# Two edits to a one-core fp32 transformer kernel: the first mixer's convolution and steps dealt anew, and the RWKV projection's third weight unit held apart

## What is computed

```python
proj = h @ w_in[l] + b_in[l]
q, k, v, gb, gc, xs = jnp.split(proj, ...)       # 512, 128, 128, 512, 512, 512 columns
q, k = rope(q), rope(k)
y_attn = sliding_window_attention(q, k, v, attn_sinks[l])   # blocks of 128, window 128, 8 heads on 2
y_conv = gc * causal_dwconv3(gb * xs, conv_w[l])            # three taps over time
y = jnp.concatenate([rms_norm(y_attn, ...), rms_norm(y_conv, ...)], axis=-1)
x = x + g1 * (y @ w_o[l])
```

## Time and profile before

| | us |
|---|---|
| median of 3 runs | 2073.39 |
| lowest, highest | 2070.76, 2075.92 |
| the profiled execution, its own time | 2070.89 |
| its span, first to last instruction | 2069.2 |
| TensorE busy in the span | 1973.0 (95%) |
| VectorE, ScalarE, GpSimd busy | 1064.3, 777.8, 252.5 |
| mean granted TensorE clock | 0.968 of full |

### The profile page before, as it was taken

The page is one execution under the profiler, slowest core; times in us unless marked ns, Lnnn a source line. Parts: engine busy times, 40 slices in busy tenths (PEclk is TensorE's granted clock), DMA queues, the critical chain, the costliest instruction groups (busy, mean ns, idle before and its releaser), DMA issues.

```text
span 2069.2 us, 35297 instructions
## 1 busy us (share of the span) xinstructions
PE 1973.0 (95%) x14503; PEld 1577.7 (76%) x14503; DVE 1064.3 (51%) x1567; ACT 777.8 (38%) x1242; POOL 252.5 (12%) x282
## 2 busy tenths in 40 slices
PE   6999899999999999799999999999989999999997
PEld 5767678888886677677777788888867878888886
DVE  6776775455324645687753744442255564444223
ACT  4333433333222335576643423222245443232221
POOL 1100000000014000322311211111100021111110
PEclk8998999999999999899999999999999999999998
DMA  8544323333332132000003133333222223333321
GB/s 309 164 132 122 92 72 93 100 92 112 101 92 73 52 92 85 6 10 7 7 27 102 44 102 98 96 113 97 81 64 79 82 72 102 92 100 100 111 84 41
DMA packets 311057, 181.09 MB, mean 88 GB/s; under 512 B 16381, under 2 KB 303763, under 8 KB 310932
## 3 DMA queue, kind: packets, MB, share of 16 engines
q1 hardware_dynamic: 305506, 162.29, 26.3%
q0 software_dynamic: 4608, 16.78, 2.6%
q10 hardware_dynamic: 818, 0.21, 0.0%
HBM read 177.16 MB, written 2.10 MB: 87 GB/s over the span
## 4 chain that ended last, share of the span: by engine, by line
PE 85%; DVE 8%; ACT 3%; issue 3%; ACTq 1%; POOL 0%; DVEq 0%; POOLq 0%
PE bank L258 22%; PE bank L260 22%; PE bank L259 22%; PE bank L2221 4%; DVE x L1399 1%; PE bank L2734 1%; ACT whi L236 1%; PE bank L1256 1%; PE bank L2728 1%; PE bank L1258 1%; PE bank L1257 1%; PE bank L562 1%; PE bank L2835 1%; DVE wlo L243 1%; PE bank L2006 1%
## 5 line engine op out<-in xcount | busy, mean ns | idle before, releaser
L243 DVE TENSOR_TENSOR wlo<-raw,whi 128x1024 fp32r<-128x1024 f32 (+1 forms) x254 | 331.1, 1304 | 665.3 <-ACT whi L236 665.1
L236 ACT ACTIVATE whi<-raw 128x1024 fp32r<-128x1024 f32 (+1 forms) x254 | 284.1, 1119 | 664.2 <-PE bank L260 657.9
L258 PE MATMUL bank<-fh_hi,whi 128*128 128x512 f32 x991 | 387.7, 391 | 0.9 <-DVE fh_lo L483 0.5
L259 PE MATMUL bank<-fh_lo,whi 128*128 128x512 f32 x991 | 386.3, 390 | 0.0
L260 PE MATMUL bank<-fh_hi,wlo 128*128 128x512 f32 x991 | 386.2, 390 | 0.0
L258 PEld LDWEIGHTS bank<-fh_hi,whi 128*128 128x128 f32 x991 | 186.4, 188 | 42.2 <-DVE fh_lo L483 1.8
L259 PEld LDWEIGHTS bank<-fh_lo,whi 128*128 128x128 f32 x991 | 186.5, 188 | 39.0 <-issue 0.5
L260 PEld LDWEIGHTS bank<-fh_hi,wlo 128*128 128x128 f32 x991 | 186.4, 188 | 38.9
L258 PE MATMUL bank<-f_hi,whi 128*128 128x512 f32 x528 | 205.7, 390 | 0.0
L260 PE MATMUL bank<-f_hi,wlo 128*128 128x512 f32 x528 | 205.4, 389 | 0.0
L259 PE MATMUL bank<-f_lo,whi 128*128 128x512 f32 x528 | 205.4, 389 | 0.0
(11 more groups left out here) (478 smaller groups left out, 3223.8 us busy)
## 6 DMA issues: line engine op xcount, KB each, us to landing
raw<-in_w_up_dram SPq DMA_DIRECT2D x44, 512.0 KB, 3.7
raw<-in_ffn_w_gate_dram SPq DMA_DIRECT2D x44, 512.0 KB, 3.7
raw<-in_ffn_w_up_dram SPq DMA_DIRECT2D x44, 512.0 KB, 3.7
raw<-in_ffn_w_down_dram SPq DMA_DIRECT2D x32, 704.0 KB, 4.2
late<-in_ada_w_dram POOLq DMA_DIRECT2D x32, 512.0 KB, 4.1
raw<-in_rwkv_w_rkv_dram SPq DMA_DIRECT2D x24, 512.0 KB, 3.4
raw<-in_w_down_dram SPq DMA_DIRECT2D x16, 704.0 KB, 4.2
early<-in_ada_w_dram SPq DMA_DIRECT2D x16, 512.0 KB, 14.2
```

What stands on the lines that cost most here:

```text
L236: act.activation(halves_of(at)[0][:, 0:kts * P], raw_unit(at, kts), ACT.Copy).then_inc(hi_ready, 1)
L243: dve.tensor_tensor(lo[:, 0:kts * P], raw_unit(at, kts), hi[:, 0:kts * P].bitcast(F32), ALU.subtract)\
L258: pe.matmul(dst, hi, rhs_hi(k), start=first and k == 0, stop=False)
L259: pe.matmul(dst, hi, rhs_lo(k), start=False, stop=False)
```

## The change

**First mixer.** (1) TensorE runs the first four tiles of unit 6 (`AHEAD`) before it transposes v and before the first scores; the wait of a group's first unit for its bank is loosened to match (`N_PRE - 1 + part`). (2) The other 92 tiles are dealt over the 16 steps by `step_start`: 5 or 6 to a step, and the third units now end 3, 2, 1 and 0 tiles before the end of steps 3, 7, 11 and 15. (3) VectorE's convolution is cut in product, taps and gate, and dealt around the next softmax: product ahead of the split; taps 0 and 1 between the softmax's first and second half; tap 2 and gate behind the second half. (4) Where a unit ends less than two tiles before its step's end (`ends_late`: steps 0, 4, 11), the low split goes behind the first half of the softmax.

**RWKV projection.** Unit 2 gets a place of its own (`w_third`, in the first half of what `y_all` kept). ScalarE splits it in the last round, behind the split of the seventh output tile; VectorE behind the last state. In `Project` the splits move up by one: at o = 0 that of unit 3 (free once unit 1 is done), at o = 1 that of unit 4 (free once unit 0 is done), none at o = 2, and the rest as before.

```diff
             elif part < 2:
-                pe.wait_ge(prj_ready, N_PRE)
+                pe.wait_ge(prj_ready, N_PRE - 1 + part)
...
     def dve_in(dve, u):
         split_lo(dve, first[u + 2])
-        at = at_in[u]
-        if u >= N_PRE and (u - N_PRE) % 3 == 2:
...
+    def conv_product(dve, j):
+        dve.wait_ge(unit_done, at_in[N_PRE + 3 * j + 2].count)
+        dve.wait_ge(gb_ready, j + 1)
+        wait(dve, conv_done, j - 1)
+        if j == 0:
+            dve.wait_ge(rope_done, 5)
+        dve.scalar_tensor_tensor(cbuf[:, j % 2, 2:T + 2], bank[MIX[2]][:, :], v("b_in", 10 + j), gb_sb[:, j % 2, :],
+                                 ALU.add, ALU.mult).then_inc(conv_p, 1)
+    def conv_tap(dve, j, w):
+        c, acc = cbuf[:, j % 2, :], cacc[:, j % 2, :]
+        if w == 0:
             dve.wait_ge(conv_p, j + 1)
+            dve.tensor_scalar(acc, c[:, 0:T], v("conv_w", j), None, ALU.mult).then_inc(conv_t, 1)
+        else:
+            dve.wait_ge(conv_t, 3 * j + w)
+            dve.scalar_tensor_tensor(acc, c[:, w:T + w], v("conv_w", 4 * w + j), acc, ALU.mult, ALU.add)\
+               .then_inc(conv_t, 1)
+    def conv_gate(dve, j):
+        dve.wait_ge(conv_t, 3 * j + 3)
+        dve.scalar_tensor_tensor(y_cv[:, j, :], bank[MIX[1]][:, :], v("b_in", 6 + j), cacc[:, j % 2, :],
+                                 ALU.add, ALU.mult).then_inc(conv_done, 1)
...
-    KS = (N_IN - N_PRE) * KD // len(STEPS)
+    AHEAD = 4
+    def step_start(i):
+        return AHEAD + ((N_IN - N_PRE) * KD - AHEAD) * i // len(STEPS)
...
-        tiles = [divmod(s, KD) for s in range(i * KS, (i + 1) * KS)]
+        tiles = [divmod(s, KD) for s in range(step_start(i), step_start(i + 1))]
...
+    def ends_late(i, u):
+        return step_start(i + 1) - (u + 1 - N_PRE) * KD < 2
...
+        pe_in(pe, N_PRE, range(AHEAD))
         pe_rotate(pe, N_PRE - 1)
         pe_scores(pe, 0)
...
         for i in range(len(STEPS)):
+            j, softmax = conv_of(i), i + 1 < len(STEPS)
+            if j is not None:
+                conv_product(dve, j)
             for u in ended(i):
-                dve_in(dve, u)
-            if i + 1 < len(STEPS):
+                if not (softmax and ends_late(i, u)):
+                    dve_in(dve, u)
+            if softmax:
                 dve_softmax_a(dve, i + 1)
+            for u in ended(i):
+                if softmax and ends_late(i, u):
+                    dve_in(dve, u)
+            if j is not None:
+                conv_tap(dve, j, 0)
+                conv_tap(dve, j, 1)
+            if softmax:
                 dve_softmax_b(dve, i + 1)
+            if j is not None:
+                conv_tap(dve, j, 2)
+                conv_gate(dve, j)
             ada_accumulate(dve, LATE_STEP[i])
...
-        sbs(part, "y_all", [P, KD, T])
+        w_third = sbs(part, "w_third", [P, 2, KD * P], F32R)
+        sbs(part, "y_late", [P, KD // 2, T])
...
                 if j:
                     act_split_y(act, j - 1)
+                if j == KD - 1:
+                    act.wait_ge(ys_ready, KD // 2)
+                    split_hi(act, out_tm.units[2], free=out_tm.at0.plus(-1))
...
                 dve_state(dve, j, 7)
+                if j == KD - 1:
+                    split_lo(dve, out_tm.units[2])
...
+        def splits_at(self, o):
+            if self.early and o < 2:
+                return self.units[o + 3], self.units[1 - o]
+            if self.early and o == 2 or o >= KD - 2:
+                return None
+            return self.units[o + 2], self.units[o]
...
             for o in range(KD):
-                at = self.at0.plus(o)
-                if o < KD - 2:
-                    split_hi(act, at.plus(2))
-                else:
+                at = self.units[o]
+                if self.splits_at(o):
+                    nxt, free = self.splits_at(o)
+                    split_hi(act, nxt, free=free)
+                if o >= KD - 2:
                     for nxt in self.after[o - KD + 2]:
                         split_hi(act, nxt, free=self.at0)
                 if o == KD - 2:
                     root_table(act)
                 act.wait_ge(unit_done, at.count)
                 if o < KD - 1:
                     act.activation(self.o[:, o, :], bank[o % 2][:, :], ACT.Copy).then_inc(o_ready.sem, 1)
```

More of the change, by code:

```diff
@@ L1030, in dve_in @@
         split_lo(dve, first[u + 2])
-        at = at_in[u]
-        if u >= N_PRE and (u - N_PRE) % 3 == 2:
[L1033 to L1041, removed]
-            dve.wait_ge(conv_p, j + 1)
-            conv_taps(dve, acc, c, lambda w: v("conv_w", 4 * w + j), conv_t, 3 * j)
-            dve.scalar_tensor_tensor(y_cv[:, j, :], bank[MIX[1]][:, :], v("b_in", 6 + j), acc,
-                                     ALU.add, ALU.mult).then_inc(conv_done, 1)
@@ L1047, in build @@
[L1047 to L1056, removed]
+    conv_t = sem("conv_t")
@@ L1198, in ended, with conv_of @@
         return [u for u, ks in pieces(i) if ks[-1] == KD - 1]
+    def ends_late(i, u):
+        return step_start(i + 1) - (u + 1 - N_PRE) * KD < 2
+    def conv_of(i):
+        return next(((u - N_PRE) // 3 for u in ended(i) if (u - N_PRE) % 3 == 2), None)
     def pe_mixer1(pe):
@@ L3103, in __init__ @@
             self.end = at0.plus(KD)
+            self.units = [at0.plus(o) for o in range(KD)]
+            if early:
+                self.units[2].held = w_third[:, 0, :], w_third[:, 1, :]
             self.o = mem
@@ L3142, in dve @@
             for o in range(KD - 2):
-                split_lo(dve, self.at0.plus(o + 2))
+                if self.splits_at(o):
+                    split_lo(dve, self.splits_at(o)[0])
             for units in self.after:
@@ L3160, in pe @@
                 if o < KD - 1:
-                    unit_products(pe, self.at0.plus(o), KD, bank[o % 2][:, :], hi, lo, True, True)
+                    unit_products(pe, self.units[o], KD, bank[o % 2][:, :], hi, lo, True, True)
             for ks in (range(KD - 1), range(KD - 1, KD)):
```

## The result

| | kernel before | changed kernel |
|---|---|---|
| median of the runs, us | 2072.06 (13 runs, 2066.73 to 2078.83) | **2054.48** (13 runs, 2049.84 to 2070.27) |
| profiled execution: its time, its span, us | 2070.89, 2069.2 | 2062.55, 2060.8 |
| ratio of the times | | **0.9923**, 95% interval 0.9908 to 0.9938 |

The change takes 17.6 us off, 0.77%. The 95% interval of the ratio stands for a gain of 12.8 to 19.1 us. The forecast was 2055.3, and its cases reached from 2050 to 2062. The profiled execution is one of the long ones of its own kernel, 8 us above its median, so its span can't be set against the other's as a whole. What can be compared is the stretch that was changed. I measure it from the first product of the last rotation to the output projection's first product: 214.90 - 84.61 = 130.29 us before, 199.02 - 88.14 = 110.88 after. **The mixer is 19.4 us shorter.**

A forecast was written before the change was run, and what follows sets the result against it. TensorE's idle and low-clock time bounds the kernel, with VectorE limiting the gain: 17.9 us in the mixer plus 0.2 in the RWKV projection, 18.1, from the median 2073.39 to 2055.3. Range 2050 to about 2058, to 2062 with half of rival 2.

The forecast's parts named there:

- The bound: First mixer: TensorE's idle and low-clock time can give back 19.9 us; VectorE, running continuously, limits the gain to 17.9.
- Four tiles ahead: First stretch, before step 0: twelve products fill 2.7 of 2.95 us idle, the clock stays high, 5.2 us gained.
- The price of 5.23 us: First stretch: twelve products at the low clock take 5.23 us and vanish; if the clock falls, only some 2.7 gained.
- VectorE's sum: First mixer: VectorE's instructions added up from softmax 2 at 100.9, less 4.7 hidden, end at 196.1; gain 17.9.
- The 2.09 from the last accumulation to the projection: Mixer's end: the output projection's first product comes 2.09 us behind the gate, as before, now at 197.0.
- Short waits of TensorE: First mixer: 2.0 us reappears as waits for probabilities and transposed copy, after steps 4, 5, 12 and 13.
- Rival 2: First mixer: the clock eats part; first stretch and short waits lose some 7 us, time 2062; chance 0.20.
- Rivals 3 and 4: Mixer: 3, probabilities stay late, no change within 0.3% (0.03); 4, waits in most steps, low clock, 2092 (0.02).
- the working on the queues: First mixer's queues: later weight loads are covered by four buffers; DMA engines busy 0.23 to 0.28 of the stalled stretches.
- Part three: RWKV projection's third unit: gain 0.2 us in place of 1.95, since unit 2 waits for bank 0's copy on ScalarE.
- The total: Whole kernel: 17.9 for the mixer plus 0.2 for the RWKV projection, 18.1 us, forecast 2055.3.

## Why the prediction was right, point by point

**The bound** was read rightly: TensorE's idle and slow time was what could be won, and VectorE's chain was what limited it. Of 4.4 us of added instructions 4.2 came through.

**Four tiles ahead.** The step "TensorE is then idle for only about 0.5 us before the scores" held: 0.40. The clock stayed at 1.00, and the slow products vanished. The stretch is as long as before (4.62 us), so all that the twelve products took later is gained. The price of 5.23 us holds only where the clock falls as it did in the first profile; without the tiles the loss was 5.3 in one place and 1.6 in a second, and in another execution of the kernel before nine products were slow and not twelve. A term of this kind has a range that one profile doesn't show.

**VectorE's sum.** From the first scores to the start of the last accumulation I had 194.9 - 89.23 = 105.7; measured, 196.94 - 92.76 = 104.2. The sum was 1.5 too long, and the gain from that profile 19.4 instead of 17.9. The mis-sized terms are these. The convolution's product is followed by an instruction that doesn't need it after 0.66 us, four times (116.03 to 116.69), where I had 0.78 from a place where the tap waits for it. Splits take 1.14 (109.59 to 110.73), not 1.18, eleven times. Together that is 0.9. What is hidden behind the exponentials is 5.2 in place of 4.7: 1.3 for the first convolution, 1.27 (not 1.0) for the second, 1.47 (not 1.25) in step 11, 1.13 for the split of step 4. Softmax 2 starts 0.16 earlier after the first scores than I had it. Against this stands 0.18 of a wait for the scores of softmax 10. That leaves 0.1. The 2.09 from the last accumulation to the projection was exact (2.08).

**Short waits of TensorE**, "a few tenths to 1.3 us each, after steps 4, 5, 12 and 13": their kind was right, and so was their sum (2.0 for p_t), but not their places. There are three, of 0.49 (at 178.67, in step 13), 0.78 and 0.69 (191.56 and 193.92, in step 15 and behind it), and none after steps 4 and 5; and the 0.69 stood in the kernel before as well. Not foreseen was the wait of 0.34 us at 123.53 for the gate (y_cv, L1058): the unit that begins with step 5 goes into the bank that the gate reads, and the gate, 122.72 to 123.47, now stands behind the softmax. I had looked at the queues behind each wait, but not at the bank that the gate holds.

**Rival 2** fell. Three pauses of 0.5 to 0.8 us and one of 0.3 lie in a stretch whose clock is 1.00; in the kernel with more vector work eight pauses, the longest 1.4, go with a clock of 0.99, which the changed kernel's own second profile shows too. What the Trainium skill ("TensorE: Matmul & The Clock Gate", section "A second HAM failure mode: psum-queue depth-cycling") reports of another kernel, that small frequent pauses between groups of products made the clock swing, does not show here at these lengths. The longer ones of the kernel before, up to 2.2, lie in stretches of low clock.

**Rivals 3 and 4** needed the probabilities to stay late. They are no longer late by more than 0.8. A reading in the working on the queues was off: the earlier trace rows has the DMA engines busy for 0.23, 0.28 and 0.12 of the three stalled stretches, not for 0.23 to 0.28, and for 0.87 of the first. Nothing hangs on it, since no wait of the steps is for a load.

**Part three** was right in its mechanism and its number: 0.2 forecast, 0.26 measured, and the copy of bank 0 named as what stands in the way, with a wait of 1.69 where 1.5 to 1.9 was forecast; 1.7 more came when it was moved.

**The total** of 18.1 against 17.6 between the medians is nearer than the reasons allow. For the profile on which it was made, the gain in the mixer was forecast 1.5 too small; but that profile's mixer is at the long end of the five, and in others the gain is up to 2.5 smaller. The two differences have opposite signs, and a cost behind the mixer, if there is one, has the sign of the second. That they nearly cancel is luck.

## What to carry to other kernels

When a wait is removed from an engine whose clock falls after it, add up the other engine's chain as well, instruction by instruction from start to start: the smaller of the two gains is the forecast, and a large part of it may be clock (10.5 of 19.4 us here). A second buffer pays only if the copy that frees the next resource does not stand behind the work that the buffer made possible; look one instruction further in that queue. And compare two kernels by the distance between two instructions of the changed stretch, in several executions, since the whole spans of the first pair show only 8.4 us of this gain.

## What the runs showed of the hardware

- **A short instruction on VectorE costs less if the next does not wait for it.** The convolution's product, 0.75 us long in both kernels, is followed after 0.78 us by the tap that reads it, and after 0.66 by an independent split (116.03 to 116.69). The copy added to VectorE is 0.42 long and took 0.34, in all 13 places.
- **The clock falls in different places in executions of one kernel.** A pause of 2.02 us was followed by scores of 0.80 us for four, or by scores of 0.49 and slow products from 93.24 to 96.89. In the kernel with the convolution in one piece it fell behind two waits of 2.18 us and not behind one of 1.62. In the kernel with the tiles behind the scores it fell a second time, at 102.58, with no pause, three products after 2.4 us of short ones. What decides this stays open.
- **Untouched code scatters by several microseconds.** The setup took 84.2 to 88.1 us in fourteen profiles, in two groups (84.2 to 85.4, and 87.2 to 88.1). This scatter of 3.9 us is 0.2% of the program, so one execution each can't tell a change of 0.1%.
